# A two-layer encoder step on one core: joined first norm, reciprocals turned by a transpose, and repeated products at four waits

## Chip, core and metric

The kernel runs on one core of a Trainium2 chip. The metric is the device time of one execution in microseconds (us). Before the change the median of three runs is 2940.51 us (2939.18 to 2941.53).

## What is computed

The reference is a streaming encoder step with two layers over 1024 prompt tokens, 16 meta tokens and 8 sample streams of 16 tokens (model width 1024, 16 heads of 64, hidden width 2816). Layer 0 attends to a sliding window with a learned sink per head, layer 1 to the 256 keys per query that an indexer selects. Each layer is a norm, projections, attention, an output projection, then a norm and a gated feed-forward network with a convolution. The parts that the change touches:

```
def rms_norm(x, g):
    y = xf * lax.rsqrt(jnp.mean(xf * xf, axis=-1, keepdims=True) + EPS)
    return (y * g.astype(jnp.float32)).astype(x.dtype)

def sink_softmax(logits, sink):
    m = jnp.maximum(jnp.max(logits, axis=-1, keepdims=True), sink)
    p = jnp.exp(logits - m)
    return p / (jnp.sum(p, axis=-1, keepdims=True) + jnp.exp(sink - m))
```

The norm's gain is multiplied in ahead of a projection, its scale behind it; the softmax is divided by its sum after the product with the values.

## The kernel before

All 1170 columns (meta, prompt, sample and two of padding) lie on the free axis, and the model width on 8 tiles of 128 partitions. Every engine has its own program, and semaphores order them.

**Products.** A projection of 128 output rows is a `gemm` on PE (L1399 and following). Operands are split in a high and a low part of fp32r, so a projection is 8 tiles x 3 products (`w_hi`,`xh`; `w_hi`,`xl`; `w_lo`,`xh`) x 3 column chunks of 390 = 72 matmuls, and its job number sets which of two PSUM tiles `ps_gemm` it fills. POOL splits each weight chunk (`split`: the copy L1190 to `w_hi`, the subtraction L1192 to `w_lo`), three chunks deep.

**Norms.** The first gemm behind a norm is gated: PE takes the `xh` products tile by tile as ACT writes the high parts (L1409), and then the `xl` products as DVE writes the low parts (`low_part`, L2178, L1414). ACT also squares every tile (L2042). The squares are added to one tile `acc`, odd tiles by POOL (`add_one`, L1204), even ones by DVE (`add_square`, L2186). `square_sum` (L1436) multiplies `acc` by a matrix of 1/1024 in three matmuls, ACT takes the root (L2045), DVE the reciprocal (`scale`, L2192). In the first norm (m=0) ACT alternates high part and square, POOL adds between the splits of chunks 0 and 1, and PE runs `square_sum` behind gemm 0. Behind gemm 1 PE turns the constants (L1644, L1648). Gemm 2 uses the PSUM tile of gemm 0 and waits until DVE has scaled it into `kt` (L2277, L2278). The norms behind the two attention stages (m=1 and 3) open the feed-forward stages. There DVE makes all eight low parts behind the last residual add, with the add of square 6 (L2186) behind low part 2; POOL adds square 7.

**Attention.** Each layer's attention runs over 73 units in a fixed order (64 pairs of heads and query tiles, and 9 for the meta tokens and streams). In step n, PE makes the scores of unit n, DVE adds bias and mask and reduces them (L2324 in layer 0, L2531 to L2559 in layer 1), ACT takes the exponential with its row sum in two calls (`probs`, L2060), and DVE the reciprocal of the two sums (L2247). Two steps later PE turns the probabilities into PSUM banks `ps_tr` in blocks of 128 (transposes, L1554). The last block of a unit, `rinv`, brings the reciprocals of both heads into the same orientation: two fp32 matmuls with 64 output rows each, whose stationary operand is a reciprocal broadcast to 64 columns (L1550). DVE and ACT copy the banks out, PE multiplies by the values (L1575, L1582), and DVE multiplies that by the turned reciprocals (L2225).

**End.** Behind the last feed-forward product PE waits for DVE's residual add, turns the result (L1954), and sums the squares with one-column matmuls (L1963, L1964).

`keep_busy` (L1531) repeats one product of `w_hi` into a bank that nobody reads. Before the change it is called ahead of two other stages only.

Of the kernel before, what the change touches and what calls it, by code (L numbers as in the profile page):

```python
# [109 lines left out]
def build(nc, a, out):  # L110

    with ExitStack() as ctx:
        def sem(name):
            return ctx.enter_context(nc.semaphore(name))
# [52 lines left out]
        for t in range(2, QT):  # L167
# [10 lines left out]
             ("low_keep", [P, 9, P], F32), ("kvtok", [P, 10, P], F32),  # L178
             ("mask_s", [P, 272], F32), ("sb_kc", [META, HD], F32), ("sb_k", [P, 2, HD], F32),
             ("sb_vc", [P, HD], F32), ("sb_v", [P, 2, HD], F32), ("kts_b", [P, 272], F32), ("qs_b", [P, P], F32),  # L180
             ("ptb_h", [P, 512], F32)],
            [("skip_scm2", [P, SCW], F32), ("skip_m02", [P, 416], F32), ("skip_sc2", [P, 288], F32),
             ("ptb_a", [P, 2, 512], F32)],
        )
# [35 lines left out]
            [("sq0", [P, T], F32), ("sq1", [P, T], F32), ("acc", [P, T], F32)],  # L220
            [("skip_t0", [P, T], F32), ("skip_t1", [P, T], F32), ("skip_t2", [P, T], F32), ("brow", [HEADS, FLEN], F32)],
            [("kt0", [P, T], F32), ("kt1", [P, T], F32), ("vf", [P, T], F32),
             ("kts_a", [P, 2, 160], F32), ("sbias_a", [P, 2, 160], F32)],
            [("skip_k", [P, 2 * T], F32), ("pta_v", [P, 2, 512], F32)],
            [("sbias_b", [P, 2, 288], F32), ("ptb_x", [P, 512], F32), ("skip_p1", [P, T - 1088], F32), ("skip_kt", [P, T], F32),
             ("xb2", [P, XBW], F32)],
# [289 lines left out]
        def stat(k, i, r=None):  # L516
            o = 6 * k + 2 * (i % 3)
            return rreg["stats"][:, o:o + 2] if r is None else rreg["stats"][:, o + r:o + r + 1]

        def near_at(i):  # L520

            t = UNITS[i]["t"]
            if t is None:
                return 512 * (i % 2)
            if t < 3:
                return 512 * (i % 2) + (P if t == 2 else 0)
            return 512 if t < 6 else P * (t - 1)
# [98 lines left out]
        first_in = sem("first_tile_bias_in")  # L626
        p_exp = sem("pair_probs_done")
        p_rinv = sem("pair_row_sum_inverse_done")
        p_tr = sem("pair_probs_transposed")
        p_ev = [sem("pair_probs_out0"), sem("pair_probs_out1")]  # L630
        p_pv = sem("pair_values_done")
# [551 lines left out]
        def _(pool):  # L1183
# [11 lines left out]
            def add_squares(m):  # L1195

                for k in range(1, KT, 2):
                    add_one(m, k)
# [103 lines left out]

            for c in range(C_WOA):
                split(c)
                if c == 0:
                    add_squares(0)
            for c in range(C_WOA, C_WOA + 3):
                split(c)

# [81 lines left out]
        def _(pe):  # L1391
            def tr_free(g):

                if g >= 2:
                    pe.wait_ge(tr_out[g % 2], g // 2)

            def gemm(c, j, x_hi, x_lo, n=P, gate=None, between=None, l=0):

                pe.wait_ge(w_split, c + 1)  # L1399
                if j >= 2:  # L1400
                    pe.wait_ge(evac[j % 2], j // 2)
                wh, wl = whi[c % 3], wlo[c % 3]
                x0, ch = X0[l], CHL[l]
                if gate is not None:
                    for k in range(KT):
                        pe.wait_ge(xh_done, gate + k + 1)
                        for w in (wh, wl):
                            for m in range(NCH):
                                pe.matmul(ps[j % 2][0:n, m, 0:ch], w[:, k, 0:n], x_hi[:, k, x0 + m * ch:x0 + (m + 1) * ch],  # L1409
                                          start=(k == 0 and w is wh), stop=False)  # L1410
                    for k in range(KT):
                        pe.wait_ge(xl_done, gate + k + 1)
                        for m in range(NCH):
                            mm = pe.matmul(ps[j % 2][0:n, m, 0:ch], wh[:, k, 0:n], x_lo[:, k, x0 + m * ch:x0 + (m + 1) * ch],  # L1414
                                           start=False, stop=(k == KT - 1))
                    mm.then_inc(mm_done, 1)
                    return
                for k in range(KT):
                    for w, x in ((wh, x_hi), (wh, x_lo), (wl, x_hi)):
                        for m in range(NCH):  # L1420
                            mm = pe.matmul(ps[j % 2][0:n, m, 0:ch], w[:, k, 0:n], x[:, k, x0 + m * ch:x0 + (m + 1) * ch],  # L1421
                                           start=(k == 0 and w is wh and x is x_hi), stop=(k == KT - 1 and w is wl))
# [105 lines left out]
                        mm = pe.transpose(tb[(g0 + gi) % 2][0:18, (f - 4 * gi) * P:(f - 4 * gi + 1) * P], cs[:, f, :], ident[:])  # L1528
                    mm.then_inc(pe_tr, 1)

            def keep_busy(slot, bank, times):  # L1531

                x = whi[slot][:].rearrange("p k n -> p (k n)")
                for _ in range(times):
                    pe.matmul(bank[:, 0:CH], whi[slot][:, 0, :], x[:, 0:CH], start=True, stop=True)

            def prompt(layer, lead, scores, keys, values, meta_values):

                def transposes(g):
                    j, i = g["j"], g["u"]  # L1540
                    if g["first"]:
                        pe.wait_ge(p_exp, 2 * (NU * layer + i) + 2)
                    if j >= 2:
                        pe.wait_ge(p_ev[j % 2], j // 2)
                    x = x_of(layer, i)
                    for k, b in enumerate(g["blocks"]):
                        if b == "rinv":
                            pe.wait_ge(p_rinv, NU * layer + i + 1)
                            for r in range(2):
                                mm = pe.matmul(tb[j % 2][HD * r:HD * (r + 1), P * k:P * (k + 1)],  # L1550
                                               stat(2, i, r).to_broadcast([P, HD]), ident[:], start=True, stop=True)
                        else:
                            c = meta_col(layer, i) if b == "meta" else xcol(layer, i, *b)
                            mm = pe.transpose(tb[j % 2][:, P * k:P * (k + 1)], x[:, c:c + P], ident[:])  # L1554
                    mm.then_inc(p_tr, 1)
# [92 lines left out]
                pe.matmul(tb[g % 2][0:HEADS, 0:FLEN], x3["tab"][:], x3["bsel"][:], start=True, stop=True).then_inc(pe_tr, 1)  # L1648


            pe.wait_ge(dve_setup, 1)
            for i, (kind, _, n) in enumerate(proj_a):
                gemm(i, J_PA + i, XH, XL, n, gate=0 if i == 0 else None)
                if i == 0:
                    square_sum(0, G_X)
                if i == 1:
                    pe.wait_ge(ss_out, 3)
                    constants()
# [283 lines left out]
                gemm(C_WOB + m_, J_WOB + m_, OH, XL, l=1)  # L1942
            ffn(C_FFB, J_FFB, 3, FT, G_CTX_B)

            for par in range(2):
                pe.wait_ge(evac[par], (J_FIN - par + 1) // 2)

# [77 lines left out]
        def _(act):  # L2025
# [3 lines left out]
            def norm(m, j_prev):  # L2029

                if m == 1:
                    act.wait_ge(stores, 16 * 22)
                for k in range(KT):
                    if m:
                        j = j_prev - KT + k
                        act.wait_ge(evac[j % 2], j // 2 + 1)
                    if m < 4:
                        copy(XH[:, k, :], h[:, k, :], gT[:, k, NORM_G[m]:NORM_G[m] + 1]).then_inc(xh_done, 1)
                    dst = x4["acc"] if k == 0 else x4["sq0"] if k % 2 else x4["sq1"]
                    if k >= 3:  # L2040
                        act.wait_ge(acc_done, 7 * m + k - 2)
                    act.activation(dst[:], h[:, k, :], ACT.Square).then_inc(sq_done, 1)  # L2042
                for i in range(NCH if m < 4 else 0):
                    act.wait_ge(ss_done, 3 * m + i + 1)
                    act.activation(R[:, i * CH:(i + 1) * CH], tb[i % 2][:, 0:CH], ACT.Sqrt, bias=eps[:, 0:1]).then_inc(ss_out, 1)  # L2045

            def prompt(layer):
# [6 lines left out]
                def probs(i, r):  # L2054
# [4 lines left out]
                    x = x_of(layer, i)[:, a:b]  # L2059
                    act.activation(x, x, ACT.Exp, bias=stat(0, i, r), scale=-1.0, accum_out=stat(1, i, r)).then_inc(p_exp, 1)  # L2060

                for n in range(NU + LAG):
                    parts = thirds(AT[layer][n])
                    part(parts[0])
                    if n < NU:
                        probs(n, 0)
                    part(parts[1])
                    if n < NU:
                        probs(n, 1)
                    part(parts[2])  # L2070
# [100 lines left out]
        def _(dve):  # L2171
# [8 lines left out]

            def add_square(m, k):

                if k and k % 2 == 0:
                    dve.wait_ge(sq_done, 8 * m + k + 1)
                    dve.wait_ge(acc_done, 7 * m + k - 1)
                    dve.tensor_tensor(x4["acc"][:], x4["acc"][:], x4["sq1"][:], ALU.add).then_inc(acc_done, 1)  # L2186

            def scale(m):
                for i in range(NCH):
# [26 lines left out]
            def prompt(layer, reduce_far, reduce_near, between):  # L2216
# [18 lines left out]
                for n in range(NU + LAG):  # L2235
# [8 lines left out]
                    part(parts[0])  # L2244
                    if 1 <= n <= NU:
                        dve.wait_ge(p_exp, 2 * (NU * layer + n))
                        dve.reciprocal(stat(2, n - 1), stat(1, n - 1)).then_inc(p_rinv, 1)  # L2247
                    if n < NU and layer == 1:
                        reduce_near(n, 0)
# [14 lines left out]

            for k in range(KT):
                low_part(0, k)
                add_square(0, k)
            scale(0)
            dve.wait_ge(const_in, 16 * N_CONST)
# [346 lines left out]
```

## Time and profile before

| What | Value |
|---|---|
| Median of three runs | 2940.51 us |
| The profiled execution: its own time / span of its instructions | 2940.25 us / 2938.4 us |
| PE busy | 2854.0 us (97%) |
| DVE / ACT / POOL busy | 1532.0 / 679.4 / 918.6 us |
| First norm, from the first high part to gemm 2 | 21.95 to 68.90 us |
| Attention of layer 0 / layer 1 | about 180 to 374 us / 1633 to 1955 us |

Busy times of PE hold the modelled latency of its pipelined matmuls, so a busy PE can still have short gaps. PE's weight loads (PEld) show the pace. The granted clock is 1.00 at 2.4 GHz and 0.50 at 1.2 GHz.

### The profile page before, as it was taken

The numbers are of one execution on the slowest core, as the hardware profiler recorded it, in microseconds if no ns is written. First come the engines' busy times: TensorE is split into PE (matmuls) and PEld (weight loads), VectorE is DVE, ScalarE is ACT, GpSimd is POOL, SyncE is SP. The second block draws the span as 40 slices with busy tenths as digits, with TensorE's granted clock in tenths as the row PEclk, the third lists the DMA queues.
The fourth block names the chain that finished last, engine by engine and source line by source line (L and its number), as shares of the span: only waits on it lengthen the run. The fifth ranks groups of instructions, "written<-read, shape, count | busy, mean of one in ns | idle before, by whom it ended". The sixth has DMA issues, their size and how long they took to land. (4 is left out here: it accounts for less than half of the span.)

```text
span 2938.4 us, 48132 instructions
## 1 busy us (share of the span) xinstructions
PE 2854.0 (97%) x18679; PEld 2687.3 (91%) x18679; DVE 1532.0 (52%) x2816; ACT 679.4 (23%) x1327; POOL 918.6 (31%) x860
## 2 busy tenths in 40 slices
PE   8999999999999999999888899999999999999998
PEld 6988899999999999998578777789999999999997
DVE  5046615554444444455588878531644444444455
ACT  4036611000000000003466655631100000000002
POOL 4233333222222222224024754323222222222221
PEclk9999999999999999999999999999999999999999
DMA  4430011111111111114012000011111111111112
GB/s 124 66 98 10 22 30 36 42 37 36 43 43 43 43 43 37 42 43 132 1 31 77 10 12 9 21 74 44 36 44 43 36 43 43 43 41 37 43 36 75
DMA packets 178206, 129.82 MB, mean 44 GB/s; under 512 B 25313, under 2 KB 168353, under 8 KB 177846
## 3 DMA queue, kind: packets, MB, share of 16 engines
q1 hardware_dynamic: 178066, 127.90, 15.4%
q8 instruction: 94, 1.54, 0.2%
q14 instruction: 46, 0.38, 0.0%
HBM read 111.13 MB, written 15.16 MB: 43 GB/s over the span
## 5 line engine op out<-in xcount | busy, mean ns | idle before, releaser
L1221 POOL CAST w_hi<-w_raw 128x1024 fp32r<-128x1024 f32 x120 | 145.2, 1210 | 1099.1 <-PE ps_gemm L1458 599.9
L668 DVE TENSOR_TENSOR h<-h,ps_gemm 128x1170 f32<-128x1170 f32 (+1 forms) x192 | 262.5, 1367 | 394.6 <-PE ps_gemm L1474 208.5
L1458 PE MATMUL ps_gemm<-xh,w_hi 128*128 128x390 f32 (+1 forms) x1920 | 445.8, 340 | 0.0
L1458 PE MATMUL ps_gemm<-xl,w_hi 128*128 128x390 f32 (+1 forms) x1920 | 444.9, 340 | 0.0
L1458 PE MATMUL ps_gemm<-xh,w_lo 128*128 128x390 f32 (+1 forms) x1920 | 444.7, 340 | 0.0
L1458 PEld LDWEIGHTS ps_gemm<-xh,w_hi 128*128 128x128 f32 x1920 | 349.2, 189 | 0.1
L1458 PEld LDWEIGHTS ps_gemm<-xl,w_hi 128*128 128x128 f32 x1920 | 348.1, 189 | 0.0
L1458 PEld LDWEIGHTS ps_gemm<-xh,w_lo 128*128 128x128 f32 x1920 | 348.0, 189 | 0.0
L1224 POOL TENSOR_TENSOR w_lo<-w_raw,w_hi 128x1024 fp32r<-128x1024 f32 x120 | 290.7, 2423 | 17.4
L676 ACT ACTIVATE ac<-ac 128x1184 f32<-128x1184 f32 x44 | 52.5, 1194 | 857.7 <-DVE ac L735 857.7
L1421 PE MATMUL ps_gemm<-xl,w_hi 128*128 128x390 f32 (+1 forms) x1056 | 246.2, 341 | 0.0
L1474 PE MATMUL ps_gemm<-gu_lo,w_hi 128*128 128x390 f32 (+1 forms) x960 | 223.4, 341 | 0.0
L1474 PE MATMUL ps_gemm<-gu_hi,w_hi 128*128 128x390 f32 (+1 forms) x960 | 222.4, 340 | 0.0
L1474 PE MATMUL ps_gemm<-gu_hi,w_lo 128*128 128x390 f32 (+1 forms) x960 | 222.0, 339 | 0.0
L713 DVE TENSOR_TENSOR ga<-ps_gemm,rms_scale 128x780 f32<-128x780 f32 (+1 forms) x44 | 42.5, 966 | 321.0 <-PE ps_gemm L1458 313.3
L2027 ACT ACTIVATE gu_hi<-gb 128x1170 fp32r<-128x1170 f32 x44 | 52.1, 1185 | 655.7 <-DVE gb L758 655.7
L1421 PEld LDWEIGHTS ps_gemm<-xl,w_hi 128*128 128x128 f32 x1056 | 193.1, 190 | 0.0
L1474 PEld LDWEIGHTS ps_gemm<-gu_lo,w_hi 128*128 128x128 f32 x960 | 174.8, 189 | 0.0
L1474 PEld LDWEIGHTS ps_gemm<-gu_hi,w_lo 128*128 128x128 f32 x960 | 174.3, 189 | 0.0
L1474 PEld LDWEIGHTS ps_gemm<-gu_hi,w_hi 128*128 128x128 f32 x960 | 173.7, 189 | 0.0
L1190 POOL CAST w_hi<-w_raw 128x1024 fp32r<-128x1024 f32 (+1 forms) x52 | 53.7, 1033 | 357.0 <-PE ps_gemm L1421 257.3
L1421 PE MATMUL ps_gemm<-xh,w_hi 128*128 128x390 f32 (+1 forms) x672 | 159.4, 345 | 3.1 <-issue 1.6
(412 smaller groups left out, 4705.7 us busy)
## 6 DMA issues: line engine op xcount, KB each, us to landing
w_raw<-in_w_gate SPq DMA_DIRECT2D x44, 512.0 KB, 3.8
w_raw<-in_w_up SPq DMA_DIRECT2D x44, 512.0 KB, 3.8
w_raw<-in_w_down SPq DMA_DIRECT2D x44, 512.0 KB, 3.5
w_raw<-in_w_in_b SPq DMA_DIRECT2D x13, 512.0 KB, 3.9
w_raw<-in_w_qkv_a SPq DMA_DIRECT2D x10, 512.0 KB, 3.9
residual_park<-h SPq DMA_DIRECT2D x1, 4680.0 KB, 13.7
h<-residual_park SPq DMA_DIRECT2D x8, 585.0 KB, 7.3
out<-yt SPq DMA_DIRECT2D x9, 512.0 KB
```

The source lines that it names most:

```text
L668: dve.tensor_tensor(c3(h[:, m, :], l), c3(h[:, m, :], l), pse(j, l), ALU.add).then_inc(evac[j % 2], 1)
L676: act.activation(ac[:, 0:GA - 2], ac[:, 0:GA - 2], ACT.Gelu_apprx_tanh).then_inc(gel_done, 1)
L713: dve.tensor_tensor(ga[:, 2 + x0:2 + x0 + 2 * ch].rearrange("p (c n) -> p c n", c=2), src[:, 0:2, 0:ch], R[:, two].rearrange("p (c n) -> p ...
L1190: pool.tensor_copy(whi[c % 3][:, :, 0:n], raw[c % 2][:, :, 0:n]).then_inc(w_hi_done, 1)
L1221: pool.tensor_copy(whi[c % 3][:], raw[c % 2][:]).then_inc(w_hi_done, 1)
L1224: pool.tensor_tensor(wlo[c % 3][:], raw[c % 2][:], whi[c % 3][:].bitcast(F32), ALU.subtract).then_inc(w_split, 1)
L1421: mm = pe.matmul(ps[j % 2][0:n, m, 0:ch], w[:, k, 0:n], x[:, k, x0 + m * ch:x0 + (m + 1) * ch], start=(k == 0 and w is wh and x is x_hi), ...
L1458: mm = pe.matmul(ps[j % 2][:, m_, 0:ch], w[:, k, :], x[:, k, x0 + m_ * ch:x0 + (m_ + 1) * ch], start=(k == 0 and w is wh and x is XH), sto ...
L1474: mm = pe.matmul(ps[(j + m_) % 2][:, i_, 0:ch], w[:, m_, :], x[:, u, x0 + i_ * ch:x0 + (i_ + 1) * ch], start=(u == 0 and w is wh and x is ...
L2027: return act.activation(dst, src, ACT.Copy, scale=scale)
```

## The change

**First norm (m=0).** ACT makes all eight high parts and then all eight squares. DVE makes all eight low parts and then adds all seven squares; POOL adds none and goes on splitting. `square_sum` stands in gemm 1, ahead of its last three products, and ahead of it 12 repeated products go to `ps_tr` bank 0.

**Norms 1 and 3.** In the gated gemm 12 repeated products go to `ps_tr` bank 0 ahead of the wait for low part 3.

**Attention, both layers.** For units 16 to 72 ACT copies the two reciprocals, each repeated 64 times, to a new tile `ri_a` or `ri_b` of 128x128 (two slots), and PE turns that with one transpose in place of the two matmuls. ACT's copy stands between the two exponentials of the next unit. DVE's reciprocal of unit n-1 waits for the copy of unit n-4 in addition.

**End.** 8 repeated products ahead of the wait for the last residual add.

```
+        WIDE = 16
+        def inverse(layer, i):
+            return (hreg["ri_b"] if layer else x4["ri_a"])[:, i % 2, :, :]
...
             def gemm(c, j, x_hi, x_lo, n=P, gate=None, between=None, l=0):
...
                     for k in range(KT):
+                        if k == 3 and gate in (KT, 3 * KT):
+                            pe.wait_ge(tr_out[0], ((G_END_A if l == 0 else G_END_B) + 1) // 2)
+                            keep_busy(c % 3, tb[0], 12)
                         pe.wait_ge(xl_done, gate + k + 1)
...
-                        if b == "rinv":
+                        if b == "rinv" and i >= WIDE:
+                            pe.wait_ge(p_wide, wide(layer, i))
+                            mm = pe.transpose(tb[j % 2][:, P * k:P * (k + 1)],
+                                              inverse(layer, i).rearrange("p r d -> p (r d)"), ident[:])
+                        elif b == "rinv":
...
+            def squares_between(k):
+                if k == KT - 1:
+                    pe.wait_ge(tr_out[0], (G_X + 1) // 2)
+                    keep_busy(1, tb[0], 12)
+                    square_sum(0, G_X)
...
-                gemm(i, J_PA + i, XH, XL, n, gate=0 if i == 0 else None)
-                if i == 0:
-                    square_sum(0, G_X)
+                gemm(i, J_PA + i, XH, XL, n, gate=0 if i == 0 else None, between=squares_between if i == 1 else None)
...
+            tr_free(G_FIN)
+            keep_busy((C_FFB + 65) % 3, tb[G_FIN % 2], 8)
...
+                def repeat_inverse(i):
+                    act.wait_ge(p_rinv, NU * layer + i + 1)
+                    if i >= WIDE + 2:
+                        act.wait_ge(p_tr, transposed(layer, i - 2))
+                    copy(inverse(layer, i), stat(2, i).unsqueeze(2).to_broadcast([P, 2, HD])).then_inc(p_wide, 1)
...
+                    if WIDE < n <= NU:
+                        repeat_inverse(n - 1)
...
+                        if n - 4 >= WIDE:
+                            dve.wait_ge(p_wide, wide(layer, n - 4))
                         dve.reciprocal(stat(2, n - 1), stat(1, n - 1)).then_inc(p_rinv, 1)
...
             for k in range(KT):
                 low_part(0, k)
+            for k in range(KT):
                 add_square(0, k)
```

PE in the first norm, before, from the end of gemm 0 (`ps_gemm0`) into gemm 1 (line numbers of the kernel before):

```order
L1414 MATMUL ps_gemm0<-xl,w_hi0 128x390 [waits x_lo_done]
L1414 MATMUL ps_gemm0<-xl,w_hi0 128x390 x2
L1436 MATMUL ps_tr0<-acc,mean_weights 128x390 [waits tr_out_act,tr_out_dve,squares_added]
L1436 MATMUL ps_tr1<-acc,mean_weights 128x390
L1436 MATMUL ps_tr0<-acc,mean_weights 128x390 [waits square_mean_root_out]
L1421 MATMUL ps_gemm1<-xh,w_hi1 128x390 [waits w_split]
L1421 MATMUL ps_gemm1<-xh,w_hi1 128x390 x2
```

And now, from the end of gemm 1 into gemm 2 (line numbers of the changed kernel, which are higher):

```order
L1410 MATMUL ps_tr0<-w_hi1 128x390 [waits tr_out_dve]
L1410 MATMUL ps_tr0<-w_hi1 128x390 x11
L1454 MATMUL ps_tr0<-acc,mean_weights 128x390 [waits tr_out_act,tr_out_dve,squares_added]
L1454 MATMUL ps_tr1<-acc,mean_weights 128x390
L1454 MATMUL ps_tr0<-acc,mean_weights 128x390 [waits square_mean_root_out]
L1439 MATMUL ps_gemm1<-xh,w_lo1 128x390 x3
L1660 MATMUL ps_tr1<-ident,crow 128x20 [waits tr_out_act,const_in,square_mean_root_out]
L1660 MATMUL ps_tr1<-ident,crow 128x20 x21
L1660 MATMUL ps_tr0<-ident,crow 128x20 [waits tr_out_dve]
L1660 MATMUL ps_tr0<-ident,crow 128x20 x21
L1664 MATMUL ps_tr1<-bsel,tab 16x384 [waits tr_out_act]
L1439 MATMUL ps_gemm0<-xh,w_hi2 128x390 [waits gemm_out0,w_split]
```

The square sums moved past 69 of the 72 matmuls of gemm 1, and 12 repeated products stand ahead of them.

PE at the end of one unit of layer 0, before (the scores of the next unit, five transposes, the reciprocals, the values):

```order
L1554 MATMUL ps_tr0<-ident,xa 128x128 [waits pair_probs_out0,pair_probs_done]
L1554 MATMUL ps_tr0<-ident,xa 128x128 x3
L1554 MATMUL ps_tr1<-ident,xa 128x128 [waits pair_probs_out1]
L1550 MATMUL ps_tr1<-ident,stats 64x128 [waits pair_row_sum_inverse_done]
L1550 MATMUL ps_tr1<-ident,stats 64x128
L1582 MATMUL ps_out<-pta_r,vtok 64x128 [waits pair_output_scaled,pair_probs_out0]
L1582 MATMUL ps_out<-pta_r,vtok 64x128 x3
```

And now PE, and below it ACT, in the same stage:

```order
L1570 MATMUL ps_tr0<-ident,xa 128x128 [waits pair_probs_out0,pair_probs_done]
L1570 MATMUL ps_tr0<-ident,xa 128x128 x3
L1570 MATMUL ps_tr1<-ident,xa 128x128 [waits pair_probs_out1]
L1561 MATMUL ps_tr1<-ident,ri_a 128x128 [waits pair_inverse_repeated]
L1598 MATMUL ps_out<-pta_r,vtok 64x128 [waits pair_output_scaled,pair_probs_out0]
L1598 MATMUL ps_out<-pta_r,vtok 64x128 x3
```

```order
L2090 ACTIVATE xa,stats<-xa,stats 128x273 [waits pair_sinks_set,pair_reduction_done]
L2050 ACTIVATE ri_a<-stats 128x128 [waits pair_probs_transposed,pair_row_sum_inverse_done]
L2090 ACTIVATE xa,stats<-xa,stats 128x273 [waits pair_reduction_done]
L2050 ACTIVATE pta_r<-ps_tr 128x512 [waits pair_values_done,pair_probs_transposed]
L2090 ACTIVATE xa,stats<-xa,stats 128x273 [waits pair_sinks_set,pair_reduction_done]
```

Two matmuls of 64 rows became one transpose of 128, with its data from ACT instead of DVE.

## Rows read from the trace of the kernel before

**Rows 1.** The page: busy time of PE, its share, instructions.

```profile
PE 2854.0 (97%) x18679; PEld 2687.3 (91%) x18679; DVE 1532.0 (52%) x2816; ACT 679.4 (23%) x1327; POOL 918.6 (31%) x860
```

**Rows 2.** Windows, layer 0 attention: length, busy PE, PEld, DVE, ACT, POOL, clock, DMA.

```profile
290.00:310.00 20.00, 20.00 (x243) 16.26 (x241) 13.42 (x55) 12.59 (x39) 7.05 (x25) 1.00 0.04 10
```

**Rows 3.** Waits of PE, 205 to 372 us: longest group (total, times, longest).

```profile
PE ps_tr L1554 <- ACT pta_v L2027: 1.1, 2, 0.8
```

**Rows 4.** Waits of PE, 1660 to 1955 us, layer 1: longest group.

```profile
PE ps_tr L1554 <- ACT ptb_a L2027: 1.7, 2, 1.3
```

**Rows 5.** Waits of ACT, 205 to 372 us: longest group.

```profile
ACT xa L2060 <- DVE stats L2324: 42.9, 53, 2.4
```

**Rows 6.** Timeline of PE's weight loads, layer 1: start, length, count, idle before.

```profile
1947.20 0.14 PEld L1554 LDWEIGHTS ps_tr<-ident,xb 128*128 128x128 f32 x1 [0.17 <-issue]
1947.46 0.20 PEld L1550 LDWEIGHTS ps_tr<-ident,stats 128*64 128x64 f32 x4
...
1948.27 0.85 PEld L1554 LDWEIGHTS ps_tr<-ident,xb 128*128 128x128 f32 x8 [0.17 <-issue]
1949.29 0.42 PEld L1582 LDWEIGHTS ps_out<-ptb_h,kvtok 128*64 128x64 f32 x8 [0.17 <-issue]
```

**Rows 7.** Timeline of ACT: two small instructions.

```profile
20.85 0.23 ACT L2027 ACTIVATE h<-ps_tr 128x64 f32<-128x64 f32 x1 [0.57 <-PE ps_tr L1634]
...
181.38 0.40 ACT L2060 ACTIVATE xa<-xa,stats 128x145 f32<-128x145 f32 x1
```

**Rows 8.** Timeline of the first norm.

```profile
21.95 1.27 ACT L2027 ACTIVATE xh<-h,gains 128x1170 fp32r<-128x1170 f32 x1 [0.88 <-DVE h L2173]
...
43.47 1.36 DVE L2186 TENSOR_TENSOR acc<-acc,sq 128x1170 f32<-128x1170 f32 x1
...
44.76 1.43 DVE L2178 SCALAR_TENSOR_TENSOR xl<-h,gains,xh 128x1170 fp32r<-128x1170 f32 x1
...
48.85 2.48 PE L1436 MATMUL ps_tr<-acc,mean_weights 128*128 128x390 f32 x6
...
49.82 2.35 POOL L1192 TENSOR_TENSOR w_lo<-w_raw,w_hi 128x1024 fp32r<-128x1024 f32 x1
...
52.23 0.80 PE L1421 MATMUL ps_gemm<-xh,w_hi 128*128 128x390 f32 x3 [0.89 <-POOL w_lo L1192]
...
57.91 1.79 DVE L2270 TENSOR_TENSOR sink_neg<-small,sink_neg 128x16 f32<-128x16 f32 x1
...
59.63 0.15 DVE L2271 TENSOR_TENSOR sink_rows<-sink_rows 128x2 f32<-128x2 f32 x1
...
61.07 1.38 DVE L2278 TENSOR_TENSOR kt<-ps_gemm,rms_scale 64x1170 f32<-64x1170 f32 x1
...
65.32 2.91 PE L1644 MATMUL ps_tr<-ident,crow 20*128 20x20 f32 x44
...
68.90 0.80 PE L1421 MATMUL ps_gemm<-xh,w_hi 128*128 128x390 f32 x3
```

**Rows 9.** Chain that ended last: start, length; one whole gemm of 72 matmuls.

```profile
2117.46 12.71 PE ps_gemm L1458 x72
```

**Rows 10.** Windows of PE alone, 1 us each: length, busy, clock, DMA.

```profile
490.00:491.00 1.00, 0.00 (x0) 0.59 0.00 0
...
497.00:498.00 1.00, 1.00 (x4) 1.00 0.00 0
...
2923.00:2924.00 1.00, 1.00 (x6) 0.56 0.00 0
```

**Rows 11.** Timeline of norm 1: PE's weight loads for the low parts.

```profile
487.64 0.48 PEld L1414 LDWEIGHTS ps_gemm<-xl,w_hi 128*128 128x128 f32 x3 [0.39 <-DVE xl L2178]
...
491.40 0.83 PEld L1414 LDWEIGHTS ps_gemm<-xl,w_hi 128*128 128x128 f32 x3 [3.28 <-DVE xl L2178]
```

**Rows 12.** Chain that ended last, at the end of the program.

```profile
2908.25 1.50 issue
...
2912.59 0.22 PE ps_far L1963 x2
...
2916.22 0.43 PE ps_far L1964 x2
```

More of the change, by code:

```diff
@@ L180, in build @@
              ("sb_vc", [P, HD], F32), ("sb_v", [P, 2, HD], F32), ("kts_b", [P, 272], F32), ("qs_b", [P, P], F32),
-             ("ptb_h", [P, 512], F32)],
+             ("ptb_h", [P, 512], F32), ("ri_b", [P, 2, 2, HD], F32)],
             [("skip_scm2", [P, SCW], F32), ("skip_m02", [P, 416], F32), ("skip_sc2", [P, 288], F32),
@@ L222, in build @@
             [("kt0", [P, T], F32), ("kt1", [P, T], F32), ("vf", [P, T], F32),
-             ("kts_a", [P, 2, 160], F32), ("sbias_a", [P, 2, 160], F32)],
+             ("kts_a", [P, 2, 160], F32), ("sbias_a", [P, 2, 160], F32), ("ri_a", [P, 2, 2, HD], F32)],
             [("skip_k", [P, 2 * T], F32), ("pta_v", [P, 2, 512], F32)],
@@ L518, in stat, with wide @@
             return rreg["stats"][:, o:o + 2] if r is None else rreg["stats"][:, o + r:o + r + 1]
+        WIDE = 16
+        def wide(layer, i):
+            return (NU - WIDE) * layer + i - WIDE + 1
+        def inverse(layer, i):
+            return (hreg["ri_b"] if layer else x4["ri_a"])[:, i % 2, :, :]
         def near_at(i):
@@ L628, in build @@
         p_rinv = sem("pair_row_sum_inverse_done")
+        p_wide = sem("pair_inverse_repeated")
         p_tr = sem("pair_probs_transposed")
@@ L1304, in _ @@
                 split(c)
-                if c == 0:
-                    add_squares(0)
             for c in range(C_WOA, C_WOA + 3):
@@ L1395, in tr_free, with keep_busy @@
                     pe.wait_ge(tr_out[g % 2], g // 2)
+            def keep_busy(slot, bank, times):
+                x = whi[slot][:].rearrange("p k n -> p (k n)")
+                for _ in range(times):
+                    pe.matmul(bank[:, 0:CH], whi[slot][:, 0, :], x[:, 0:CH], start=True, stop=True)
             def gemm(c, j, x_hi, x_lo, n=P, gate=None, between=None, l=0):
@@ L1529, in ctx_transposes @@
                     mm.then_inc(pe_tr, 1)
[L1531 to L1535, printed above, removed]
             def prompt(layer, lead, scores, keys, values, meta_values):
@@ L2032, in norm, with high_part @@
                     act.wait_ge(stores, 16 * 22)
+                def high_part(k):
+                    copy(XH[:, k, :], h[:, k, :], gT[:, k, NORM_G[m]:NORM_G[m] + 1]).then_inc(xh_done, 1)
+                if m == 0:
+                    for k in range(KT):
+                        high_part(k)
                 for k in range(KT):
@@ L2036, in norm @@
                         act.wait_ge(evac[j % 2], j // 2 + 1)
-                    if m < 4:
-                        copy(XH[:, k, :], h[:, k, :], gT[:, k, NORM_G[m]:NORM_G[m] + 1]).then_inc(xh_done, 1)
+                    if 0 < m < 4:
+                        high_part(k)
                     dst = x4["acc"] if k == 0 else x4["sq0"] if k % 2 else x4["sq1"]
@@ L2181, in add_square @@
             def add_square(m, k):
-                if k and k % 2 == 0:
+                if k and (k % 2 == 0 or m == 0):
                     dve.wait_ge(sq_done, 8 * m + k + 1)
-                    dve.wait_ge(acc_done, 7 * m + k - 1)
-                    dve.tensor_tensor(x4["acc"][:], x4["acc"][:], x4["sq1"][:], ALU.add).then_inc(acc_done, 1)
+                    if k > 1:
+                        dve.wait_ge(acc_done, 7 * m + k - 1)
+                    dve.tensor_tensor(x4["acc"][:], x4["acc"][:], x4["sq1" if k % 2 == 0 else "sq0"][:], ALU.add).then_inc(acc_done, 1)
             def scale(m):
@@ L2266, in _ @@
                 low_part(0, k)
+            for k in range(KT):
                 add_square(0, k)
```

## Prediction

> **What bounds the kernel now.** Start with the page's busy times: PE is busy for 2854.0 of 2938.4 us [rows 1], so only what shortens PE's own work, or a wait of PE, can move the time by much. Then read the windows of the attention stages, where the change does most. In layer 0 PE is busy in all 20.00 us of a window at granted clock 1.00, ACT in 12.59 and DVE in 13.42 [rows 2]. A busy PE may hide short waits, so read its list of waits: the longest group of layer 0 is 1.1 us in 167, the longest of layer 1 1.7 us in 295 [rows 3, 4]. ACT in turn waits 42.9 us in layer 0 for DVE's reductions [rows 5]. Attention is bound by the number of passes that PE makes.
>
> The first norm is different. From 21.95 to 68.90 us PE is held by others in turn. Gemm 1 starts only at 52.23, behind POOL's split of its weights, which POOL does behind its adds, and gemm 2 at 68.90 [rows 8].
>
> **Turned reciprocals.** Units 16 to 72 are 57 per layer, 114 in all. Read PE's weight loads near the end of layer 1 [rows 6]. From the reciprocals (1947.46) to the next transposes (1948.27) are 0.81 us. That holds 4 passes of reciprocals, 8 of values and an idle 0.17, so a pass takes (0.81 - 0.17) / 12 = 0.053 and the reciprocals 4 x 0.053 = 0.213. The 8 transposes at 1948.27 take 1.02 with the idle 0.17 behind them, so one takes 0.85 / 8 = 0.106. The idle 0.17 stands wherever PE goes from 128-row to 64-row blocks or back. Before, that is between transposes and reciprocals; now it is between the new transpose and the values. It is paid once either way. A unit saves 0.213 - 0.106 = 0.107 us, and 114 units 12.2 us.
>
> ACT gets 114 copies of 128x128. The nearest rows are 0.23 us (64 columns) and 0.40 (145 columns) [rows 7], so some 0.3 each. The page "ScalarE: Activation LUTs" of the Trainium skill (section "What ACT_TABLE_LOAD costs") gives 186 ns + 0.833 ns per column for such an instruction, which would be 0.29, an estimate, and the sum would not change. Cost on the path: nothing. The copy runs while ACT would wait for the second reduction (42.9 us over 53 waits, 0.81 each [rows 5]), and DVE issues the reciprocal ahead of that reduction. Without that cover it would cost up to 0.40 - 0.107 = 0.29 a unit. Behind the copy on ACT are the second exponential and copies out of PSUM, whose reader is PE one or two steps later. DVE's added wait is for a copy three units old. Bounds of this term: -12.2, or half of it (-6) if every second unit is limited by something other than PE. I take -12.2, since PE waits for almost nothing [rows 3, 4].
>
> **The first norm.** ACT's eight high parts take at most 8 x 1.27 [rows 8] and end near 32. POOL splits chunk 1 from 22 on, so gemm 1 finds its weights. DVE's low parts take 8 x 1.43 = 11.4 from 23.3 on, plus one stand behind POOL's subtraction of 2.35, and end at 37. PE starts at half clock and keeps it for some 6 us: after norm 1's pause it restarted at 491.40 and was at full clock again by 497 [rows 10, 11]. That allows three tiles of high-part products until 29.4. The other five are 30 matmuls of 12.71 / 72 = 0.177 [rows 9], until 34.7, and 24 low-part products end near 39. Then 69 matmuls of gemm 1 reach 51.3. DVE's seven adds take 7 x 1.36 = 9.5, from 37 to 46.5, or to 51.2 if two of POOL's subtractions hold them. So the squares are ready when PE comes, and the 12 repeated products (12 x 0.177 = 2.1) cover no wait but push the square sums to 53.4. Before, they began at 48.85 and DVE had freed the PSUM tile of gemm 0 at 61.07 + 1.38 = 62.45: 13.6 us, of which 1.64 were a small DVE instruction held (1.79 against 0.15 for the next). POOL is idle at that time now, so 12.0 remain, and gemm 2 starts at 65.5 in place of 68.90: -3.4.
>
> But PE has nothing to do from about 60.4 until 65.5: the square sums and roots take up to 52.23 - 48.85 = 3.4 from 53.4 on, the constants 68.90 - 65.32 = 3.6 [rows 8]. A shorter pause, 3.28 us in norm 1, brought the clock down to half (0.59 over the microsecond from 490 on, 1.00 again from 497 [rows 10, 11]), and it stayed there 5.6 us beyond the restart. At half pace gemm 2 loses 5.6 / 2 = 2.8. I take -3.4 + 2.8 = -0.6; ends -3.4 (clock held) and +2 (squares another 2.6 late).
>
> **The waits of norms 1 and 3.** PE stands 3.28 us for low part 4 [rows 11], which DVE starts late because POOL's add of square 7 holds it. The 12 products (2.1) go ahead of low part 3 and push only products that fit into that pause: cost nothing, or +2.1 each if the pause were gone. If they hold the clock, the last three low-part products take 0.48 instead of 0.83 [rows 11] and the square sums gain as much: -0.7 each. But behind them PE again works for 0.48 and waits for DVE in turn, so the clock may fall later and reach into gemm 1, at up to half of 2.8, +1.4 each. The two are about as likely and I take 0 for both norms; ends -1.4 and +2.8.
>
> **The end.** PE idles 1.50 us ahead of the last transposes [rows 12], and 8 products are 1.4: free, at most +0.1. The loss of clock there comes later, in the one-column sums: pairs of 0.22 become 0.43, and the clock is back near 2923.6 [rows 10, 12]. Ten such pieces lose 2.1, and I allow 1 more for the transposes behind them. Since what runs when the clock falls is unchanged, I take 0; the ends are -3 and +0.1.
>
> **Sum.** -12.2 - 0.6 + 0 + 0 = -12.8 on the profiled execution's 2940.25, which is 2927.4. That run lies 0.26 below the median of three, so 2927.7.
>
> **The rivals.**
> - *PE is only partly the bound.* The reciprocals give half, -6.1 - 0.6: 2933.8. For: the busy PE is a modelled figure, and each step is shortened for PE alone. Against: rows 3 and 4. Chance 0.15.
> - *The clock stays up everywhere.* -12.2 - 3.4 - 1.4 - 3 = -20: 2920.5. For: four stretches of repeated products. Against: in the first norm they stand ahead of the long pause, not in it. Chance 0.10.
> - *ACT becomes the bound (slower).* Its copy in each of 114 units sits ahead of an exponential and a copy out of PSUM. If nothing covers it, 114 x (0.3 - 0.107) = +22: 2962. It decides once ACT's idle time per unit falls below the copy's 0.3; now it is 0.81 in each of 53 waits [rows 5]. Chance 0.04.
> - *The new wait costs an idle stretch of its own*, so the change of block size is not merely moved: 114 x (0.17 - 0.107) = +7, less 0.6: 2947. Against: the 8 transposes at 1948.27 are two groups with a wait each and run in 0.85 without a gap [rows 6]. Chance 0.04.
> - *The clock falls in attention.* There the share of transposes grows and that of matmuls shrinks; each fall would cost 2.8, so from the fifth on nothing is gained, and 20 falls make 2983. Against: around 2923.6, where PE runs transposes alone, the clock rises to full [rows 10]. Chance 0.02. This is what "TensorE: Matmul & The Clock Gate" of the Trainium skill would make of it: in its section on transposes it says that transpose mode doesn't count as PE-busy for the clock. The trace disagrees at the end of this program.
>
> **How the numbers follow.** My forecast gets 0.65. About 0.2% (5.9 us) is what a measurement of this kernel tells from no change. Faster by more: the forecast, the held clock and 0.09 of the first rival, 0.84. Within: 0.06 of it and half of the new wait, 0.08. Slower: the rest, 0.08. The range 2920 to 2935 holds the forecast with the ends of its smaller terms (0.62 of 0.65), the held clock (0.09), and the better part of the first rival (0.09).
>
> **What would show it.** Right: each step of attention from unit 16 on is 0.1 us shorter, PE's waits in attention stay a few us, 114 copies of about 0.3 us stand in ACT's idle time; gemm 1 starts near 39, the square sums near 53, gemm 2 near 65.5 at half clock. Wrong: PE waiting for `ri_a` or for ACT's copies by more than 0.1 us a unit, an idle stretch on both sides of the new transpose, square sums that wait for the adds, or a gemm behind norm 1 or 3 at half clock.

## The result, and the profile after

The changed kernel takes 2923.95 us (median of 4, 2920.72 to 2925.08) where the kernel before takes 2940.36: a ratio of 0.9943, 95% interval 0.9927 to 0.9959. Five more executions of each gave 2922.48 and again 0.9943 (0.9929 to 0.9957). That is faster, inside the range of 2920 to 2935, and about 4 us under the forecast of 2927.7.

The page's first line, which answers to [rows 1]: TensorE's busy time and the span fell by about as much (18.6 and 17.1 us).

```profile
span 2921.3 us, 47865 instructions
...
PE 2835.4 (97%) x18381; PEld 2671.8 (91%) x18381; DVE 1538.3 (53%) x2820; ACT 700.5 (24%) x1441; POOL 909.3 (31%) x856
```

A window in layer 0's attention, as in [rows 2], shows PE still busy throughout at full clock, and ACT with 14.64 us of work where it had 12.59.

```profile
280.00:300.00 20.00, 20.00 (x233) 16.15 (x233) 13.90 (x56) 14.64 (x50) 7.04 (x25) 1.00 0.04 10
```

The new tile of layer 1 by itself (operation, count, shortest/median/longest ns): 57 copies of 0.296 us, and 57 transposes. Nothing in the view of the tile names PE as standing idle for it.

```profile
L2050 ACT ACTIVATE ri_b<-stats x57: 291/296/307, 1657.3 to 1930.8; 128x128 f32<-128x128 f32 x57
L1561 PEld LDWEIGHTS ps_tr<-ident,ri_b x57: 139/142/144, 1659.0 to 1936.1; 128*128 128x128 f32 x57
```

PE's weight loads in the same unit as [rows 6]:

```profile
1931.18 0.14 PEld L1570 LDWEIGHTS ps_tr<-ident,xb 128*128 128x128 f32 x1 [0.17 <-issue]
1931.24 0.14 PEld L1561 LDWEIGHTS ps_tr<-ident,ri_b 128*128 128x128 f32 x1
1931.55 0.42 PEld L1598 LDWEIGHTS ps_out<-ptb_a,kvtok 128*64 128x64 f32 x8 [0.17 <-issue]
1932.14 0.86 PEld L1570 LDWEIGHTS ps_tr<-ident,xb 128*128 128x128 f32 x8 [0.17 <-issue]
```

From 1931.18 to 1932.14 are 0.96 us; the same stretch took 1948.27 - 1947.20 = 1.07 before. Ahead of the four reciprocals PE's weight loads stood idle for 0.12 us (1947.46 - 1947.34); that is gone, and an idle of 0.17 now stands ahead of the values instead: one such gap in either order.

The first norm in time order, against [rows 8]:

```profile
21.44 9.41 ACT L2050 ACTIVATE xh<-h,gains 128x1170 fp32r<-128x1170 f32 x8 [0.89 <-DVE h L2211]
...
35.70 13.60 DVE L2225 TENSOR_TENSOR acc<-acc,sq 128x1170 f32<-128x1170 f32 x7
...
40.20 2.22 POOL L1201 CAST w_hi<-w_raw 128x1024 fp32r<-128x1024 f32 x1 [13.75 <-DMA w_raw<-in_w_qkv_a]
...
48.85 2.30 PE L1410 MATMUL ps_tr<-w_hi 128*128 128x390 f32 x12
...
50.99 2.42 PE L1454 MATMUL ps_tr<-acc,mean_weights 128*128 128x390 f32 x6
...
63.05 1.31 PE L1439 MATMUL ps_gemm<-xh,w_hi 128*128 128x390 f32 x3 [5.32 <-DVE kt L2320]
```

Gemm 2 starts at 63.05, not 68.90. Its first three products take 1.31 us, those at 69.01 0.69: it begins at half clock, as forecast. Three windows of the clock (the third figure from the end). The first is of the kernel before, at gemm 0. The others are of the changed kernel: the clock stayed up at gemm 0, and it was down at gemm 2.

```profile
20.00:30.00 10.00, 7.71 (x31) 6.24 (x29) 6.08 (x5) 8.55 (x10) 4.90 (x2) 0.66 0.28 28
```

```profile
20.00:30.00 10.00, 7.85 (x45) 6.88 (x46) 8.15 (x6) 8.78 (x9) 6.37 (x3) 1.00 0.29 29
...
60.00:70.00 10.00, 6.95 (x24) 6.98 (x25) 4.27 (x5) 0.00 (x0) 0.00 (x0) 0.55 0.07 22
```

In the second profile of the changed kernel the clock was down at gemm 0 as well, and the prediction's times (53.4 for the sums, 65.5 for gemm 2) are met to 0.2 us:

```profile
24.23 1.18 PE L1424 MATMUL ps_gemm<-xh,w_lo 128*128 128x390 f32 x3
...
35.84 15.59 DVE L2225 TENSOR_TENSOR acc<-acc,sq 128x1170 f32<-128x1170 f32 x7
...
53.29 2.42 PE L1454 MATMUL ps_tr<-acc,mean_weights 128*128 128x390 f32 x6
...
65.36 1.31 PE L1439 MATMUL ps_gemm<-xh,w_hi 128*128 128x390 f32 x3 [5.11 <-DVE kt L2320]
```

**The account by stage.** Marks are starts of PE's products in the timeline, and the times are us. Each kernel was profiled twice, in different executions.

| stretch | before | before, 2nd | after | after, 2nd | difference of means |
|---|---|---|---|---|---|
| start to the end of layer 0's projections | 172.11 | 173.45 | 168.88 | 170.60 | -3.0 |
| to the scores of unit 12 | 37.11 | 34.76 | 33.18 | 33.14 | -2.8 |
| to norm 1's gemm (attention, output projection) | 267.98 | 268.01 | 261.93 | 261.93 | -6.1 |
| norm 1's gemm and sums | 21.55 | 21.55 | 20.90 | 22.03 | -0.1 |
| layer 1's preparation, after the first FFN | 274.76 | 274.81 | 277.66 | 275.88 | +2.0 |
| layer 1's attention | 322.37 | 322.39 | 317.11 | 317.11 | -5.3 |
| output projection and norm 3 | 123.66 | 123.65 | 124.01 | 122.79 | -0.3 |
| end (from the last transposes on) | 28.65 | 28.71 | 27.45 | 27.00 | -1.5 |

The two FFN stretches, 859.3 and 830.9 us, agree to 0.1. (Unit 12 is the first stream unit, whose scores read `qs_a`. The expectations below call this mark unit 9: counted by the scores, it is unit 12.)

### The profile page after: what moved, and what is told of

Same layout as the page of the kernel before. It is cut to its first block and busy times, and to the rows that moved or that the text cites. A ratio compares the mean times of both kernels' runs of the same rounds, so it can differ in the third digit from the quotient of the medians.

```text
span 2921.3 us, 47865 instructions
## 1 busy us (share of the span) xinstructions
PE 2835.4 (97%) x18381; PEld 2671.8 (91%) x18381; DVE 1538.3 (53%) x2820; ACT 700.5 (24%) x1441; POOL 909.3 (31%) x856
## 6 DMA issues: line engine op xcount, KB each, us to landing
residual_park<-h SPq DMA_DIRECT2D x1, 4680.0 KB, 13.7
```

## The experiments

**Second profiles of both kernels**, unedited. For the kernel before:

> The kernel before, once more, to see what differs between two executions of the same program. My theory: the stretches that are not disturbed repeat to 0.1 us (267.98 from unit 9 of layer 0 to norm 1's gemm, 322.37 from layer 1's first unit to its output projection), while where the clock falls in the first norm, ahead of and in layer 0's first units (37.1 us from the last gemm of layer 0's projections to unit 9) and in layer 1's preparation moves by 1 to 3 us. Rival (the falls belong to the kernel): all stretches repeat to 0.3 us.

Measured: 2939.3. Attention repeats to 0.03 us and layer 1's preparation to 0.05 (274.81), the latter against my theory; the stretch ahead of unit 12 moved by 2.35 and the first one by 1.3. For the changed kernel:

> The changed kernel once more, to have its median from as many executions as its variants have. My theory (its executions differ by where the clock falls): a median between 2921 and 2925, with a spread of 4 to 6 us, and attention's undisturbed stretches equal to the first profile's to 0.1 us (261.93 in layer 0 from unit 9 on, 317.11 in layer 1). Rival (the first four executions were lucky): 2926 to 2928, nearer to the prediction.

Measured: 2922.48 (2920.21 to 2925.03). Attention repeats to 0.01 us and the stretch ahead of unit 12 to 0.04; the first stretch, norm 1, layer 1's preparation and norm 3 differ by 1.1 to 1.8. So attention's gain belongs to the kernel. For a stretch that moves between two executions, one pair of profiles can't say how much belongs to the kernel.

**The turned reciprocals alone** (the first norm as before, no new repeated products; against the changed kernel, in short):

```diff
             for c in range(C_WOA):
                 split(c)
+                if c == 0:
+                    add_squares(0)
...
-            tr_free(G_FIN)
-            keep_busy((C_FFB + 65) % 3, tb[G_FIN % 2], 8)
```

> The kernel before with the turned reciprocals alone. My theory (the turned reciprocals shorten TensorE's path by 0.107 us a unit; where the clock falls elsewhere differs a little from one kernel to the next): 12.2 us under the kernel before, so about 2928, with the stretch of layer 0's attention from unit 9 on to the output projection 6.0 shorter and layer 1's 5.3 to 6.1 shorter; the first norm as before (gemm 2 near 68.9). Rival (PE only partly the bound, and the clock gave the rest): 6 us under it, 2934.

Measured: 2926.35 (2925.83 to 2928.24), ratio 0.9956 (0.9943 to 0.9970): 13.7 us under the kernel before. Unit 12 to norm 1 took 261.92 and layer 1's attention 317.18, the changed kernel's values. Gemm 2 started at 68.84. Attention gives 11.3 of the 13.7, and 11.3 of the 16.4 of the whole change; the rest of the 13.7 is in stretches whose instructions are those of the kernel before (the one ahead of unit 12 took 33.22). All nine executions of the changed kernel lie under all five of this one, so the other parts of the change are worth something together, some 2 to 4 us in medians. The complement, those parts without the turned reciprocals, has no measurement: as it was written, its engines would have waited for one another without end. This profile also shows a loss in layer 1's preparation. There PE stands for a copy of ACT that comes behind a step of the search for the best keys, which runs on DVE and ACT, and a small instruction of that search differs. By shape, here and in the changed kernel:

```profile
L2493 DVE SCALAR_TENSOR_TENSOR small<-small 128x6 f32<-128x6 f32 x2 | 0.3, 166 | 0.2
```

```profile
L2506 DVE SCALAR_TENSOR_TENSOR small<-small 128x6 f32<-128x6 f32 x2 | 4.4, 2202 | 0.2
```

In the changed kernel the timeline has POOL's subtraction ahead of it by 0.29 us, and it ends only after that:

```profile
1491.69 2.41 POOL L1203 TENSOR_TENSOR w_lo<-w_raw,w_hi 128x1024 fp32r<-128x1024 f32 x1
...
1491.98 2.14 DVE L2506 SCALAR_TENSOR_TENSOR small<-small 128x6 f32<-128x6 f32 x1
```

**ACT's copy, and nearly as much again**:

```diff
+                    copy((hreg["ri_d"] if layer else x4["ri_c"])[:], stat(2, i).unsqueeze(2).to_broadcast([P, 2, 40]))
                     copy(inverse(layer, i), stat(2, i).unsqueeze(2).to_broadcast([P, 2, HD])).then_inc(p_wide, 1)
```

> The changed kernel with a second copy on ACT ahead of each of the 114 (80 columns, about 0.25 us, into a place that nobody reads). My theory: in layer 0 ACT still waits 28.7 us in 54 waits, so the stretch from unit 9 to norm 1's gemm grows by less than 0.5 us; in layer 1, where 0.8 us of the gain were already lost to waits for ACT's and DVE's results, it grows by 1 to 3: in all 1 to 3.5 above the changed kernel. Rival (ACT is nearly the bound): 114 x 0.25 = 28 above it. Rival (ACT has time everywhere): within 0.7.

Measured: 2921.55 (2918.41 to 2926.12), not above the changed kernel. The added copies took 0.256 us each:

```profile
L2050 ACT ACTIVATE ri_d<-stats x57: 251/256/267, 1651.3 to 1925.1; 128x80 f32<-128x80 f32 x57
```

Layer 0's stretch stayed at 261.93, layer 1's grew from 317.11 to 317.43. So 29 us of added work cost 0.3 in attention: "ACT has time everywhere" holds, and my 1 to 3 us for layer 1 were too many.

**Turned from unit 3 on** (and without the first norm's products):

```diff
-        WIDE = 16
+        WIDE = 3
```

> The kernel without the 12 products of the first norm, with the reciprocals turned from unit 3 on instead of unit 16: 26 more units. My theory: each is worth 0.106 us where PE is the bound, which in layer 0 it is from about unit 9 on (7 of the 13) and in layer 1 nearly everywhere (13): 20 x 0.106 = 2.1 under the kernel without the 12 products, about 2920.4. Rival (the early units wait for ACT and DVE, and the copies make that worse): equal to it or up to 2 slower.

Measured: 2933.92 (2931.18 to 2936.07), 13.5 us above what I expected, and my theory falls. The stretch ahead of unit 12 took 41.31 us (33.17 with units from 16 on) and layer 1's attention 319.93. PE's waits in the first 47 us of attention, and there the first of them:

```profile
PE ps_tr L1561 <- ACT ri_a L2048: 3.4, 3, 1.6
```

```profile
184.12 0.42 ACT L2088 ACTIVATE xa<-xa,stats 128x145 f32<-128x145 f32 x1 [2.01 <-POOL xa L1276]
...
184.53 0.29 ACT L2048 ACTIVATE ri_a<-stats 128x128 f32<-128x128 f32 x1
...
184.87 0.14 PEld L1561 LDWEIGHTS ps_tr<-ident,ri_a 128*128 128x128 f32 x1 [1.58 <-ACT ri_a L2048]
```

ACT's order puts the copy behind an exponential of the next unit, which waits 2.01 us here, for POOL's copy into `xa`, while PE in these short units already stands at the transpose. PE waits 3.4 us, and its clock, which is up here in the changed kernel, has a mean of 0.53 from 186 to 204. Most of the rest of the 8.1 goes with that; the two were not separated. So a wait for the new tile does cost time, but in the early units, which the change leaves out.

**Turned from unit 10 on**, with the same line:

> The changed kernel with the reciprocals turned from unit 10 on instead of unit 16: 6 more units per layer. My theory (from unit 10 on the copy is done before TensorE comes for it, before that TensorE waits for it): 12 x 0.106 = 1.3 us under the changed kernel, with the stretch of layer 1's attention 0.6 shorter than the changed kernel's 316.56. Rival (the early units' waits reach beyond unit 10): 0 to 3 us above the changed kernel.

Measured: 2920.88 (2920.07 to 2926.75), ratio 0.9937 (0.9924 to 0.9951), not told apart from the changed kernel's. The stretches: 0.5 shorter in layer 0 (261.44), 0.5 longer in layer 1 (317.57). The gain of 1.3 that I expected is not there: what layer 0 wins, layer 1 loses.

**No repeated products at all:**

```diff
-                            keep_busy(c % 3, tb[0], 12)
...
-                    keep_busy(1, tb[0], 12)
...
-            keep_busy((C_FFB + 65) % 3, tb[G_FIN % 2], 8)
```

> The changed kernel without its four stretches of repeated products. My theory: in the first norm the products cost about 1.5 us (the adds end at 49.30 and the products hold the square sums until 50.99), in norm 1 they saved 0.7 and at the end about 1, in norm 3 nothing: the sum is near 0, 2923 to 2925, with the clock down at norm 1 as it was before. Rival (the products hold the clock and that is worth most of what the prediction did not see): 4 us or more slower than the changed kernel, 2928 or more.

Measured: 2925.16 (2923.22 to 2928.50), ratio 0.9953 (0.9939 to 0.9966); its interval overlaps the changed kernel's, so the two are not told apart. Norm 1 took 22.03 us, the end 30.51.

**Without those of the first norm alone:**

> The changed kernel without the 12 repeated products of the first norm alone. My theory: DVE's adds end near 49.4 as before, and the square sums follow at once, not at 50.99, so gemm 2 starts 1.4 us earlier, near 61.6, again at half clock: 1.4 us under the changed kernel, 2922.5. Rival (the clock falls elsewhere instead and takes it back): within 0.7 us of the changed kernel or slower.

Measured: 2920.0 (median of five, 2918.35 to 2924.66; a sixth execution took 11346.8 us and is left out), ratio 0.9933 (0.9920 to 0.9946). That is 2.5 to 4 us under the changed kernel's medians, but the intervals overlap, and the profile doesn't show the reason that I gave: there the seven adds took 15.59 us again, the square sums waited for them until 52.44, and gemm 2 started at 64.61, between the 63.05 and 65.36 of the changed kernel. How long the adds take (13.60 and 15.59 us, where 7 x 1.36 would be 9.5) moves the sums about as far as the products do (2.1).

**Products in the pause ahead of gemm 2:**

```diff
-                    keep_busy(1, tb[0], 12)
...
                     constants()
+                    tr_free(G_LOAD)
+                    pe.wait_ge(w_split, 3)
+                    keep_busy(2, tb[G_LOAD % 2], 28)
```

> The changed kernel with the 12 products of the first norm taken out and 28 put behind the constants, into the pause in which PE stood idle from 57.7 to 63.05 ahead of gemm 2. My theory: the square sums start near 49.4, gemm 2 near 61.5 and at full clock, so 1.5 + 2.9 = 4.4 us under the changed kernel: 2919.5. Rival (the clock falls later by itself, whatever fills this pause, or the products delay gemm 2): within 1.5 us of the changed kernel, or slower.

Measured: 2924.64 (2920.90 to 2929.90), no gain. The timeline:

```profile
51.95 3.27 PE L1454 MATMUL ps_tr<-acc,mean_weights 128*128 128x390 f32 x6 [2.26 <-DVE acc L2226]
...
59.87 6.81 PE L1410 MATMUL ps_tr<-w_hi 128*128 128x390 f32 x28
...
62.60 1.38 DVE L2321 TENSOR_TENSOR kt<-ps_gemm,rms_scale 64x1170 f32<-64x1170 f32 x1
...
66.51 0.70 PE L1439 MATMUL ps_gemm<-xh,w_hi 128*128 128x390 f32 x3
```

PE had stood 2.26 us for the adds, and the clock was down for part of the products: 28 take 5.0 us at full clock, here 6.81. DVE had freed the tile at 63.98, but the products held gemm 2 until 66.51. It then ran at full clock. The whole first stretch took 169.62 (168.88 and 170.60 in the changed kernel): what the clock gave, the delay took.

**POOL's split held back, and the sums earlier.** The adds share their time with POOL's splitting of chunks that are needed only later:

```diff
             for c in range(C_WOA):
+                if c == 2:
+                    pool.wait_ge(acc_done, 7)
                 split(c)
...
-                if k == KT - 1:
-                    pe.wait_ge(tr_out[0], (G_X + 1) // 2)
-                    keep_busy(1, tb[0], 12)
+                if k == KT - 2:
                     square_sum(0, G_X)
```

> The changed kernel without the 12 products of the first norm, with POOL's split of chunk 2 held back until DVE's seven adds are done, and the square sums after the seventh tile of gemm 1 instead of the eighth's low-part products. My theory (the adds, which ended between 49.3 and 52.4 in the runs so far, are held by POOL's casts and subtractions): the adds run at 1.4 to 1.5 us each from 35.7 and end near 46, the square sums start near 47, gemm 2 near 59 and at half clock as before: 4 us under the changed kernel, 2920. Rival (the adds are slow by themselves, or the clock takes the gain back): the square sums again at 49 or later, within 1 us of the changed kernel.

Measured: 2916.65 (2915.93 to 2919.0), ratio 0.9922 (0.9908 to 0.9935). Run with the changed kernel's second set (2920.21 to 2925.03), every execution lies under all of that one's.

```profile
36.56 10.27 DVE L2225 TENSOR_TENSOR acc<-acc,sq 128x1170 f32<-128x1170 f32 x7
...
46.89 1.04 POOL L1201 CAST w_hi<-w_raw 128x1024 fp32r<-128x1024 f32 x1 [19.58 <-DVE acc L2225]
...
49.55 2.42 PE L1456 MATMUL ps_tr<-acc,mean_weights 128*128 128x390 f32 x6
```

The seven adds take 10.27 us, POOL's cast 1.04 instead of 2.22. The sums start at 49.55, not at the 47 of my theory: the adds had ended at 46.83, and PE came only then. In its profile every stretch but the first agrees to 0.1 us with that of the kernel without the first norm's products alone; the first took 166.97 against 169.99. Of these 3.0, 1.29 is PE's wait for the adds, which is gone, and most of the rest is the earlier place of the sums, which the shorter adds allow; the two edits were not run apart. This version beats both kernels. With units from 10 on as well:

> Both of these edits together. My theory: their sum, 5 us under the changed kernel, about 2919. Rival: the clock takes part of it back, 2921 to 2923.

Measured: 2916.86 (2914.28 to 2921.77): nothing more.

**The same without the products of norms 1 and 3 and of the end:**

> The kernel with POOL's split held back and the early square sums, now without the repeated products of norms 1 and 3 and of the end too. My theory (norm 1's stretch took 20.9 to 22.8 us with them and 21.6 to 22.0 without, norm 3's 122.8 to 124.4 with and 123.7 to 124.0 without, the end 27.0 to 30.5 with and 27.8 to 30.5 without: by single profiles they are worth nothing at norm 1 and under 1 each at norm 3 and the end): 0 to 2 us above the kernel with them, 2917 to 2919. Rival (the 4 us between the kernel without any and the one without the first norm's alone were theirs): 2920 to 2921. Rival (they cost time): under 2916.

Measured: 2921.89 (2919.40 to 2923.48), ratio 0.9941 (0.9927 to 0.9955): 5.2 above the kernel with them, and nearer to the rival than to my theory. But the two were run at different times (the kernel before took 2939.34 and then 2940.17), their intervals overlap, and the two profiled executions differ by 0.4 only (2919.0, the slowest of the one, and 2919.4, the fastest of the other): norm 3's stretch took 123.95 (122.79 with the products), the end 27.42 (27.01), norm 1 22.03 (22.09), the first stretch 165.86 (166.97). What the products are worth, and in which stage, is open.

## Why the prediction was right, point by point

**Turned reciprocals, -12.2: measured -11.3.** Layer 0 gave 6.05 us for 57 units, 0.106 each, the predicted value, and from unit to unit its lead over the kernel before grows by just that. Layer 1 gave 5.3: most of its units gain as much, a few gain nothing, and some 0.8 are missing. PE's waits in layer 1's attention sum to 5.3 us now and to 5.1 before, so they show only a part of that. Groups of these waits, first now and then before:

```profile
PE ps_tr L1570 <- ACT ptb_a L2050: 1.9, 3, 1.0
...
PE ps_far L1931 <- DVE stats L2601: 0.7, 3, 0.4
...
PE ps_tr L1570 <- ACT ptb_x L2050: 0.2, 1, 0.2
```

```profile
PE ps_tr L1554 <- ACT ptb_a L2027: 2.2, 3, 1.3
...
PE ps_far L1910 <- DVE stats L2559: 0.5, 3, 0.2
```

The group of `ps_far` grew and that of `ptb_x` is new: there PE, coming earlier, now stands for another engine. It is what the prediction's lower bound (-6) allowed for, in a few units and not in every second. The first group fell, and where the rest of the 0.8 went is open. "ACT hides the copies" is shown by the doubled load. The rival with PE only partly the bound (-6.1) falls with the turned reciprocals alone.

**The clock in attention.** The rival that it falls there failed: the window above has 1.00, and no profile of the changed kernel shows a fall from unit 12 on in either layer's attention. The rule in "TensorE: Matmul & The Clock Gate" of the Trainium skill (section "Part 4: PE-mode transpose"), by which transposes don't count as busy, finds no support here, though a stretch in which other products run too can't refute it.

**First norm, -0.6: measured -3.0 between the means.** The steps were right in order: gemm 2 came at 63.05 and 65.36 (65.5 forecast) and began at half clock. One length was wrong: the seven adds took 13.60 and 15.59 us, not 9.5, and in the second profile ended at 51.43, later than the latest end that I allowed (51.2). It cost nothing only because PE came to the products at 51.16, so that the match of 65.36 is in part luck. The term was too small because I took the clock of one execution for the kernel's. Against the profile that I read, the two profiles after gain 3.2 and 1.5; the second profile before ended the projections 1.3 later. And the half clock at gemm 0, which I kept, was absent in one of the two profiles after.

**The first units: forecast nothing, measured -2.8.** In the kernel before the clock falls once more in the first units, in both profiles, and in neither of the changed kernel's. The windows of before and after at the same work:

```profile
192.00:200.00 8.00, 6.82 (x46) 5.42 (x46) 4.52 (x22) 2.88 (x12) 2.58 (x9) 0.58 0.15 39
```

```profile
189.00:197.00 8.00, 7.52 (x89) 6.02 (x86) 4.94 (x26) 5.28 (x19) 3.60 (x13) 1.00 0.18 47
```

These units were not changed. With the turned reciprocals alone the fall is gone too (33.22 us); with the products ahead of gemm 2 it is back (35.09), and with units from 10 on too (34.94). What decides it was not found. That the sum took every stretch that the change leaves alone at nothing is the weakest step of the prediction: there the clock's falls move too. The total stayed in the range because the reciprocals came out nearly as forecast and because the misses of this and the other stretches (-2.4, -2.8, +2.0, -1.5) cancel in part, which is luck.

**Layer 1's preparation: forecast nothing, measured +2.0.** I read PE's views alone, but here PE stands for the search. Its wait ahead of the transposes of `kt`, now and before:

```profile
PE ps_tr L1866 <- ACT kvtok L2050: 15.3, 1, 15.3
```

```profile
PE ps_tr L1845 <- ACT kvtok L2027: 11.3, 1, 11.3
```

POOL's subtractions now meet a two-input instruction of the search and hold it (0.17 becomes 2.2 us), twice in this stretch, and the wait is 4.0 us longer. The Trainium skill's "SBUF — State Buffer" (section "Who interferes with whom") calls what these two share an exclusive lock; the trace agrees: the small instruction ends right behind the subtraction. That the stretch lost only 2.9 and 1.1 is because PE reached this wait 1.2 and 2.9 us earlier. And the sign isn't settled by it: with ACT's copies doubled and with products ahead of gemm 2 the two instructions were held as long, and the stretch took 271.38 and 271.43, less than in the kernel before.

**Norms 1 and 3, 0: measured -0.1 and -0.3.** In the first profile norm 1's clock stayed up and 0.65 were gained, in the second it fell (0.66 in the mean from 482 to 487) and 0.48 were lost: of the two cases that the prediction weighed, each occurred once, the loss a third of the allowed 1.4.

```profile
482.00:487.00 5.00, 4.20 (x11) 2.58 (x10) 1.92 (x2) 0.40 (x1) 1.46 (x2) 0.66 0.00 0
```

**The end, 0: measured -1.5.** "What runs when the clock falls is unchanged" failed. In the changed kernel the fall comes later among the one-column sums, so fewer of them are slow:

```profile
2892.19 1.61 PE L1410 MATMUL ps_tr<-w_hi 128*128 128x390 f32 x8
...
2898.34 0.36 PE L1986 MATMUL ps_far<-mean_weights,acc 128*128 128x1 f32 x2
2898.56 0.54 PE L1987 MATMUL ps_far<-mean_weights,sq 128*128 128x1 f32 x2
```

Before, the first slow pair came 5.3 us behind the last product (2913.57 - 2908.25), now 6.2 (2898.56 - 2892.35); without any repeated products it came ahead of the sums in one profile, and the end took 30.51. But that the eight products delay it is not shown: over all profiles the end took 27.00 to 30.43 with them (30.43 with products ahead of gemm 2) and 27.42 to 30.51 without.

## What to carry to other kernels

Where PE is busy throughout, count its passes: one 128-row transpose for four 64-row passes was worth its 0.106 us a unit in layer 0, and 0.093 in layer 1, where a few units gain nothing, in both profiles. Such a change stops paying where the engine isn't the bound: in the early units the copy's wait, and the clock that fell behind it, cost 0.4 us a unit ((41.31 - 33.17 + 319.93 - 317.11) / 26). Before crediting or blaming an edit for a few us, profile each kernel twice and compare stage by stage; a stretch that differs between two executions of one kernel is no evidence by itself.

## What was not expected

- A delay of work that nobody waits for can be a gain: holding POOL's split back shortened DVE's seven adds from 13.6 us or more to 10.3. With the first norm's products out and the sums one tile earlier as well, the time fell by 5.8 (2922.48 to 2916.65); without those products alone it was 2920.0.
- POOL's cast, with one operand in SBUF, is slowed by DVE's adds too: 1.04 us alone, 2.22 beside them.
- Filling PE's pause with products doesn't by itself keep the clock at 2.4 GHz: behind a wait of 2.26 us they ran partly at 1.2 GHz and delayed the work behind them.
